# Filling a routed-token buffer with zeros by a memory-to-memory copy instead of stores from SBUF

## The reference

```python
def _block(x, state, p):
    h = _rmsnorm(x, norm_mix_w)
    proj = h @ w_in
    qkv, z, a, b, u, gate_a, gate_b = jnp.split(proj, cuts, axis=-1)
    qkv, conv_new = _causal_conv(qkv, conv_buf, conv_w)
    ...
    o, s_new = _gated_delta(q, k, v, g, beta, s_delta)
    y_a = o @ w_a_up
    ys, hr_new, hi_new = _s5(u, h_re, h_im, ...)
    y_b = ys @ w_b_up
    mixed = (sigmoid(gate_a) * y_a + sigmoid(gate_b) * y_b) @ w_o
    x = x + mixed
    x = x + _hier_moe(_rmsnorm(x, norm_ffn_w), w_rc, w_rf, w_eu, w_ed)
```

## Time and profile before

| what | value |
|---|---|
| median of three executions | 1700.71 us |
| the profiled execution | 1700.71 us |
| its span, first to last instruction | 1698.9 us |
| TensorE busy | 1517.6 us, 89% of the span |
| VectorE, ScalarE, GpSimd busy | 737.5, 396.7, 207.8 us |
| moved by DMA | 273.25 MB, 161 GB/s over the span |
| TensorE's share of the chain that ended last | 72% |

### The profile page before, as it was taken

The page is one execution under the profiler, slowest core; times in us unless marked ns, Lnnn a source line. Parts: engine busy times, 40 slices in busy tenths (PEclk is TensorE's granted clock), DMA queues, the critical chain, the costliest instruction groups (busy, mean ns, idle before and its releaser), DMA issues.

```text
span 1698.9 us, 16119 instructions
## 1 busy us (share of the span) xinstructions
PE 1517.6 (89%) x6083; PEld 949.4 (56%) x6083; DVE 737.5 (43%) x1295; ACT 396.7 (23%) x639; POOL 207.8 (12%) x224
## 2 busy tenths in 40 slices
PE   8999999989898989599999599999939999999960
PEld 6676666546655656356889466555424444444430
DVE  4657865013343322786776323244532321121118
ACT  3211101116565564231311500011101111111103
POOL 0000100000000000254277000001110000000014
PEclk9999999999999999799999799999969999999985
DMA  5273864414311112424201622223278999999937
GB/s 160 77 128 117 252 204 105 143 52 115 88 52 27 39 27 80 105 63 134 67 1 29 262 94 77 66 87 136 102 258 292 370 373 366 365 373 367 367 133 281
DMA packets 226021, 273.25 MB, mean 161 GB/s; under 512 B 62420, under 2 KB 158024, under 8 KB 225680
## 3 DMA queue, kind: packets, MB, share of 16 engines
q1 hardware_dynamic: 198388, 203.54, 38.2%
q10 hardware_dynamic: 18140, 34.48, 5.3%
q0 software_dynamic: 9408, 34.08, 5.2%
HBM read 188.83 MB, written 83.24 MB: 160 GB/s over the span
## 4 chain that ended last, share of the span: by engine, by line
PE 72%; DVE 10%; ACT 8%; issue 5%; POOL 2%; DMA 2%; ACTq 1%; POOLq 0%; DVEq 0%
PE P L677 21%; PE P L1114 12%; PE P L1065 7%; PE P L1023 7%; PE P L1098 6%; POOL arena L587 2%; PE P L834 2%; PE P L858 2%; PE P L1085 2%; DVE arena L1404 1%; DVE arena L1478 1%; PE P L703 1%; PE P L809 1%; DMA arena<-y_d,arena 1%; PE P L1045 1%
## 5 line engine op out<-in xcount | busy, mean ns | idle before, releaser
L677 PE MATMUL P<-arena 128*128 128x352 f32 (+1 forms) x1728 | 542.2, 470 | 0.0
L677 PEld LDWEIGHTS P<-arena 128*128 128x128 f32 (+1 forms) x1728 | 327.1, 193 | 185.5 <-issue 28.6
L1114 PE MATMUL P<-arena 128*128 128x512 f32 x512 | 227.2, 597 | 0.8 <-ACT arena L2143 0.8
L1114 PEld LDWEIGHTS P<-arena 128*128 128x128 f32 x512 | 95.7, 192 | 109.5 <-issue 109.5
L1065 PE MATMUL P<-arena 128*128 128x512 f32 (+1 forms) x288 | 128.9, 597 | 1.9 <-DVEq L1562 1.9
L1023 PE MATMUL P<-arena 128*128 128x352 f32 x384 | 115.7, 465 | 8.6 <-DVE arena L1548 8.6
L1706 DVE COPY arena<-P 128x512 f32<-128x512 f32 x32 | 22.1, 691 | 220.3 <-PE P L1085 220.3
L1098 PE MATMUL P<-arena 128*128 128x512 f32 x256 | 115.3, 593 | 0.9 <-DVE arena L1740 0.9
L1023 PEld LDWEIGHTS P<-arena 128*128 128x128 f32 x384 | 74.0, 193 | 50.9 <-issue 11.1
L587 POOL TENSOR_TENSOR arena<-arena,N 64x256 f32<-64x256 f32 x96 | 79.1, 824 | 49.8 <-ACT arena L2078 26.9
L1065 PEld LDWEIGHTS P<-arena 128*128 128x128 f32 (+1 forms) x288 | 50.2, 181 | 62.3 <-issue 59.7
(11 more groups left out here) (393 smaller groups left out, 1877.6 us busy)
## 6 DMA issues: line engine op xcount, KB each, us to landing
arena<-in_w_expert_up_dram SPq DMA_DIRECT2D x32, 2048.0 KB, 13.0
arena<-in_w_expert_down_dram SPq DMA_DIRECT2D x32, 1024.0 KB, 7.4
arena<-in_w_in_dram SPq DMA_DIRECT2D x36, 512.0 KB, 4.1
x_d<-zero SPq DMA_DIRECT2D x4, 4096.0 KB, 20.0
arena<-x_d POOLq DMA_DIRECT2D x32, 512.0 KB, 5.8
y_d<-arena ACTq DMA_DIRECT2D x32, 512.0 KB, 7.9
gate_d<-arena ACTq DMA_DIRECT2D x16, 528.0 KB, 4.5
arena<-gate_d SPq DMA_DIRECT2D x16, 528.0 KB, 4.5
```

The source lines that it names most:

```text
L677: m = pe.matmul(P[0:p, b + j, 0:TBK], w[:, k, 0:p], hT[:, k, TBK * j:TBK * j + TBK], start=f, stop=l)
L1114: m = pe.matmul(P[:, i % 2, :], xgT[i % 2][:, k, :], WU[i % NWE][:, k, :], start=k == 0, stop=k == KD - 1)
```

## The change

The four stores of zeros to `x_d` behind the loads of jobs 9 to 12 are gone from SP's program. The clearing of `y_d` stays where it is; its helper is written out in place. POOL, after the masking of the pair matrix (L550), now waits until all eight parts of `y_d` are zero, and then issues two copies from memory to memory, each of 8 MB, from the 2048 zero rows of `y_d` into one half of `x_d`. They count on the semaphore `s_sct`, which the scatter to `x_d` waits for, and whose later count is raised by 32. ACT waits for `y_d` alone.

```diff
-        X_PARTS, Z_PARTS = 4, 8
+        Z_PARTS = 8
...
             pool.affine_select(out=NA, in_=NA, compare_op=ALU.is_ge, fill=NEG, base=-1, pattern=[[1, C], [-1, C]],
                                channel_multiplier=0).then_inc(s_pairm, 1)
+            pool.wait_ge(s_yz, 1 + 16 * Z_PARTS)
+            half = E * 128 // 2
+            for b in range(2):
+                pool.dma_start(x_d[half * b:half * b + half, :], y_d[128 * E:128 * E + half, :]).then_inc(s_sct, 16)
             for hp in range(HP):
                 pool.wait_ge(s_sel, hp + 1)
...
-            pool.wait_ge(s_yz, 1 + 16 * (X_PARTS + Z_PARTS))
+            pool.wait_ge(s_sct, 32)
             for i in range(TT_):
...
-            act.wait_ge(s_yz, 1 + 16 * (X_PARTS + Z_PARTS))
+            act.wait_ge(s_yz, 1 + 16 * Z_PARTS)
             expert_tiles(act, run)
...
             for n in range(8, J_Y + 3):
                 weights(n)
-                if 9 <= n < 9 + X_PARTS:
-                    part = E * 128 // X_PARTS
-                    cleared(x_d[part * (n - 9):part * (n - 8)], part)
...
                 if lo == E:
-                    sp.wait_ge(s_sct, 16 * 2 * TT_)
+                    sp.wait_ge(s_sct, 32 + 16 * 2 * TT_)
```

More of the change, by code:

```diff
@@ L2263, in _ @@
                     first = 128 * E + part * (n - AB - 1)
-                    cleared(y_d[first:first + part], part)
+                    sp.wait_ge(s_yz, 1)
+                    sp.dma_start(y_d[first:first + part].rearrange("(p t) d -> p (t d)", p=128).rearrange("p (a b) -> p a b", b=128),
+                                 zero[:].unsqueeze(1).broadcast_to([128, part * D // 128 // 128, 128])).then_inc(s_yz, 16)
                 if n == AB + 3:
```

## The result

The changed kernel takes 1729.07 us (median of 4 runs, 1724.17 to 1730.26) beside 1701.20 us for the kernel before (4 runs, 1700.43 to 1702.35). The ratio is 1.0157, with a 95% interval of 1.0137 to 1.0178: 28 us slower, where +10.7 us was forecast. The profiled execution took 1730.11 us with a span of 1728.4 us, 29.5 us more than the span before.

A forecast was written before the change was run, and what follows sets the result against it. TensorE was taken to bound the kernel. 0 (removal) + 0 (POOL) + 10.7 us (ACT behind kk_d) raised the span from 1698.9 to 1709.6, with 1.8 around it 1711.4 us (chance 0.40); range 1699.8 to 1745.

The forecast's parts named there:

- Removal 0: Four 4 MB stores at 153 to 235 us: dropping them gives 0, at most the one 0.5 us wait of TensorE.
- POOL 0: On POOL, the wait for y_d and two copy issues cost 0, vanishing in 189.81 us idle before the decay mask.
- Copy 45.3 us: 16.78 MB copy at 370 GB/s, 2.83 us per 64 KB piece, running from 500.9 to 546.2 us.
- qs_d delayed by 14 us: Sample rows' send at 505.82 loses 14 us beside the copy, lands at 521.2, before its buffer is wanted at 525.34.
- 4 to 10 pieces a turn: kk_d's send at 523.89 passes 28 to 70 of 133 packets per engine in 7 turns, so lands at 548.7 us.
- What that wait costs: ACT waits from 534.69 to 548.7 for kk_d's staging buffer; 10.7 us of it reaches TensorE's transposes.
- second rival: Send of qs_d at 505.82 lands only at the copy's end, stopping ACT from 525.34; about 1722 us, chance 0.08.
- 3.3 us hidden: Of ACT's wait from 534.69, 3.3 us are hidden because TensorE's next transposes into that bank start at 538.29.
- Nothing of it comes back: After the 10.7 us wait, later stages are bound by TensorE, so everything behind moves by one constant.
- Rival 1: Queues share time fairly, kk_d lands within 14 us and nothing waits; 1700.2 to 1700.7 us, chance 0.37.
- Rival 3: Copy runs at only 210 to 185 GB/s, ending at 581 to 592 us; 1725 to 1757 us, chance 0.10.
- rival 4: Stores at 153 to 235 us did cost over 3.4 us of waits; 1696 us or less, chance 0.05.

The follow-up runs named there:

- the two kernels without the held issue: Changed kernel with ScalarE sending the convolution rows ahead of kk_d: 1719.83 us; changed kernel with that convolution-rows send left out: 1721.63 us.

## Why the prediction was wrong in size

Its direction was right, and the time lies in the range it gave. By its steps:

- **Removal 0: right.** The copy made on top of the stores costs as much as in their place; the stretch answering has 25.00 of 25.00 us both times.
- **POOL 0: right.** The two issues take 1.28 us, and 215.86 us of idle time follow.
- **Copy 45.3 us: too short.** A piece takes 3.06 us on average, not 2.83, so 16 of them take 49 us, and the engines do not keep step: the first piece starts at 501.8 us and the last ends at 553.3, 51.5 us or 326 GB/s. The end is 7.1 us later than forecast (546.2). The estimate from the "HBM Reference" page of the Trainium skill (46.9 us) was nearer, and still 4.6 us short.
- **qs_d delayed by 14 us: nearly.** 13.4 us to landing against 15.4. The steps by packets were right for a send with few pieces. **w_in in time: right**, 36.0 us, before 568.84.
- **kk_d "4 to 10 pieces a turn": the reading of the earlier trace rows failed, without a price.** The measured number is one (74, 74 and 73 packets). A window of the kernel before in which both queues have work throughout would have told: here is its DMA by queue from 1388.9 to 1390.9 us,

```profile
q0 software_dynamic: 132, 0.49, 60.0%
q1 hardware_dynamic: 115, 0.25, 47.5%
```

  nearly one for one, where 1388 to 1390 gave 79 to 269, because q0 had work in only a part of that window. The landing came at 555.5 us (523.9 + 31.6) instead of 548.7, but these 6.8 us are those of the copy's later end (7.1): kk_d was through 2.2 us behind that end, where the prediction had put 2.5. (Among its signs it writes "near 20 us" for this landing; its own sum gives 24.8.) With that landing the prediction's own sum gives a wait of 17.5 us instead of 10.7, and the two kernels without the held issue show 19 and 22.
- **The failed step that decides the size is "What that wait costs": "ACT stands there until 548.7", from 534.69.** ScalarE stands from 526.04, at the issue of the next send, until 553.70. Of the 16.3 us missing (27.0 less 10.7), 7.9 are the earlier start (what stands behind the held issue began at 526.77 before, the read of the sample rows at 534.69), 5.0 the later end (553.7 against 548.7), and 3.3 what was to be hidden. The prediction knew a slow queue as a late landing only. It had the right line in its second rival (ScalarE stopped at the convolution rows' send at 525.34, about 1722 us, given 0.08), but for a reason that did not happen: it blamed the landing of qs_d, which was in time.
- **3.3 us hidden: wrong here**, since the hold begins before TensorE's own work runs out; where the landing wait stands alone, 20.26 us on ScalarE become 15.99 on TensorE, so 4.3 are hidden there, and 2.1 where the send is left out (23.64 to 21.5).
- **"Nothing of it comes back", one constant behind: right** (+27.04, +27.29, +27.3). The clock fell to 0.55 and 0.50 in 530 to 560 us, and to 0.92 behind it (0.96 in the 40 us from 533 of the kernel before, which answer to them). What that cost was not tested apart.
- **Rival 1 (fair shares)** needed kk_d to land within 14 us: 31.6. **Rival 3 (slow copy, 80 to 91 us)** and **rival 4 (stores cost something)** are excluded by the copy's 51.5 us and by the kernel with both.
- **That the range held is luck.** It reached to 1745 us for the sake of rival 3, a slow copy; the measured 1729.07 us lies in it for another reason. The sum's own forecast gave 1704.5 to 1720.

Still open: how many entries ScalarE's queue holds. The issue is held for long behind two DMAs of 1024 pieces, for 3.4 us at most behind one, and it is let go when between 449 and 838 of their packets have moved; no kernel varied kk_d's own number of pieces. Nor did a kernel send packets smaller than 4 KB from the copy.

## What to carry to other kernels

A transfer is hidden by idle bandwidth only if no queue with many small pieces must pass it: count the packets of the other queues in its time and give each a whole turn of the large piece. Then look at what stands behind those issues on the issuing engine; an issue that is a little longer than its twins (1.08 against 0.59 us) may be the first sign of such a hold, and an engine held there stands for everything behind it, with no landing wait in the code. Count packets in the trace and not pieces in the code: 8192 pieces of 1 KB were 2048 packets of 4 KB. Here a wait that starts the copy after the many-pieced send makes it free, but also useless: ask first whether the transfer that is moved was costing anything where it stood.

## What the runs showed of the hardware

- Queues that have work on the same DMA engines take turns of one packet, software against hardware queue and hardware against hardware alike: 74/74/73 with 64 KB pieces, 1060/1063 with 4 KB. A 64 KB piece is one closed turn (3.06 us on average). The rule of the Trainium skill weighed in rival 1 (page "DMA: Bandwidth & Descriptors", section "SWDGE vs HWDGE vs iDMA", a packet of preferably at most 4096 B) does not bound a turn in these traces: the 64 KB piece is one packet. With pieces of 1 KB the packets are 4 KB, which agrees with it.
- A DMA issue can hold the issuing engine while earlier DMAs of its own queue are not through: 27.61 us on ScalarE, 29.67 us on POOL.
- A copy from memory to memory ran at 326 GB/s in 64 KB pieces, over its 51.5 us (343 GB/s in 520 to 530 us at a DMA share of 1.02, so each byte moved counts once), beside the 367 of the earlier trace rows.
- A stand of TensorE of 31.5 us brought TensorE's granted clock to 0.55 and 0.50, the 1.2 GHz level, and the next 40 us had 0.92.
